# Hybrid decoder step with routed experts on one core: output products by column halves, the first expert's rows picked by TensorE products

## What is computed

```python
x = x + merged @ w['w_out']
hn = rms_norm(x, w['norm_ffn_g']).reshape(B * S, D_MODEL)
x = x + hier_moe(hn, ...)         # every token goes to the best 2 experts of the best of 4 groups
# hier_moe, per expert e, on the rows sent to it:
#   yp = (silu(xb @ w_gate[e]) * (xb @ w_up[e])) @ w_down[e]
#   out[token] += yp * weight of (token, expert)
```

## Time and profile before

| | |
|---|---|
| median of 3 runs | 1033.21 us (1033.18 to 1034.37) |
| the profiled execution | 1037.51 us |
| its span, first to last instruction | 1035.7 us |
| PE busy | 903.2 us, 87% of the span |
| DVE, ACT, POOL busy | 365.3, 224.0, 85.9 us |
| read from HBM, written | 252.46 MB, 14.58 MB |

### The profile page before, as it was taken

One profiled execution on the slowest core, in us unless ns is written; L12 is line 12 of the kernel. 1 busy time (PEld: TensorE's weight loads), 2 busy tenths in 40 slices (PEclk: granted clock), 3 DMA queues, 4 the chain that ended last, 5 costly groups with the idle time before them and its releaser, 6 DMA issues.

```text
span 1035.7 us, 11180 instructions
## 1 busy us (share of the span) xinstructions
PE 903.2 (87%) x4299; PEld 507.1 (49%) x4299; DVE 365.3 (35%) x806; ACT 224.0 (22%) x570; POOL 85.9 (8%) x89
## 2 busy tenths in 40 slices
PE   6899799999899999999859999787877788778784
PEld 5454677777678888755423433232332333233331
DVE  4588568767353345534414111111110101111010
ACT  3432354364622100032201111000010100001010
POOL 0100000000000000000011122010111011010111
PEclk9999899999999999999959999989999999999998
DMA  8622212112112228096369999999999999999991
GB/s 309 205 82 85 77 41 84 46 42 82 41 41 81 82 82 275 1 396 284 125 250 405 389 395 394 388 415 395 404 398 406 407 401 408 402 413 397 411 395 47
DMA packets 34095, 258.46 MB, mean 250 GB/s; under 512 B 9000, under 2 KB 12328, under 8 KB 18792
## 3 DMA queue, kind: packets, MB, share of 16 engines
q1 hardware_dynamic: 28000, 244.93, 59.4%
q0 software_dynamic: 6048, 12.89, 4.7%
HBM read 252.46 MB, written 14.58 MB: 258 GB/s over the span
## 4 chain that ended last, share of the span: by engine, by line
PE 55%; DMA 26%; DVE 7%; issue 6%; ACT 4%; SPq 1%; another core or an unknown queue 1%; POOL 0%; POOLq 0%; DVEq 0%; ACTq 0%
DMA arena<-in_w_gu 19%; PE ps L1723 19%; PE ps L1996 12%; PE ps L2015 7%; PE ps L1662 6%; DMA arena<-in_w_ed 5%; PE ps L1880 4%; PE ps L1985 2%; DVE arena L1289 1%; ACT arena L825 1%; DVE a_stat L1315 1%; DMA arena<-in_x_T 1%; DVE arena L1312 1%; DMA hn_rows<-arena 1%; ACT arena L837 1%
## 5 line engine op out<-in xcount | busy, mean ns | idle before, releaser
L1723 PE MATMUL ps<-arena 128*128 128x272 f32 x1120 | 269.4, 397 | 13.4 <-ACT arena L725 5.8
L1996 PE MATMUL ps<-arena 128*64 128x512 f32 x512 | 232.8, 603 | 19.7 <-DMA arena<-in_w_gu 19.5
L1723 PEld LDWEIGHTS ps<-arena 128*128 128x128 f32 x1120 | 209.9, 191 | 65.1 <-ACT arena L725 11.5
L1997 PE MATMUL ps<-arena 128*64 128x512 f32 x512 | 233.0, 603 | 0.0
L2015 PE MATMUL ps<-arena 128*64 128x512 f32 x512 | 134.6, 673 | 57.2 <-issue 44.0
L725 ACT ACTIVATE arena<-ps 128x272 f32<-128x272 f32 (+5 forms) x172 | 77.2, 457 | 401.5 <-PE ps L2015 175.3
L1996 PEld LDWEIGHTS ps<-arena 128*64 128x64 f32 x512 | 67.0, 138 | 156.1 <-issue 123.8
L1521 DVE SCALAR_TENSOR_TENSOR arena<-ps,list_w,arena 64x512 f32<-64x512 f32 x32 | 23.8, 743 | 286.5 <-ACT arena L990 286.5
L2015 PEld LDWEIGHTS ps<-arena 128*64 128x64 f32 x512 | 43.7, 153 | 145.8 <-issue 137.0
L1662 PE MATMUL ps<-arena 128*128 128x512 f32 (+1 forms) x192 | 75.6, 552 | 8.1 <-DMA arena<-in_w_kv 7.1
L685 POOL DMA_INDIRECT out_y<-arena,list_i x32 | 45.6, 1426 | 402.9 <-PE ps L1985 342.7
(11 more groups left out here) (224 smaller groups left out, 692.1 us busy)
## 6 DMA issues: line engine op xcount, KB each, us to landing
arena<-in_w_gu SPq DMA_DIRECT2D x64, 2048.0 KB, 48.6
arena<-in_w_ed SPq DMA_DIRECT2D x32, 2048.0 KB, 51.2
arena<-in_w_pair SPq DMA_DIRECT2D x20, 1024.0 KB, 4.8
arena<-in_x SPq DMA_DIRECT2D x8, 512.0 KB, 8.2
arena<-in_w_q SPq DMA_DIRECT2D x2, 2048.0 KB, 16.5
arena<-in_w_out SPq DMA_DIRECT2D x2, 2048.0 KB, 13.4
arena<-in_x_T SPq DMA_DIRECT2D x4, 512.0 KB, 8.9
out_y<-arena SPq DMA_DIRECT2D x4, 512.0 KB, 7.0
```

The lines of the kernel that those rows point to most:

```text
L1723: ins = mm(out, w[:, k, :], tokens[:, k, :], start=k == 0 and q in "127", stop=k == 3, skip_group_check=q not in "127")
L1996: mm(ps[0:C, 2 + s, :], xT[s][:, j, :], w[:, jj, 0, :], start=j == 0, stop=j == JX - 1)
L1997: ins = mm(ps[64:64 + C, 2 + s, :], xT[s][:, j, :], w[:, jj, 1, :], start=j == 0, stop=j == JX - 1)
```

## The change

- `w_out` comes as two contiguous column halves. PE does the first column halves of tiles 0 to 3 (h = 1 to 4), then the second halves (h = 5 to 8); the parts of a half are 2, 2 and 4 products (turn, route between them). The routing products of the first halves go to PSUM regions of their own and are kept in `part_logits` (one DVE copy); `choice` adds the second halves' to them.
- The buffer of chunk 7 is the first half of `w_out`: SP loads it when the first halves are done, chunk 8 when all are, chunk 9 after the last rows' transfers. The last tile's write to `hn_rows` moves from POOL's queue to SP's, behind chunk 8. The decode rows of x get a place of their own (part of `const`), so that all of x is loaded beforehand.
- Expert 0's rows are no longer gathered. `hits` makes for each tile a 128x64 table `pick_at` (row r, place p: the row's 1/rms where r belongs at place p of expert 0, else 0), and PE multiplies x by it, 8 products a tile into one PSUM bank that 4 products with a zero row have cleared (`clear_rows`, `pick_rows`). The sum is expert 0's rows, turned and normalised. Counts and the list of weights move to between the two halves of `gate_up(0)`; `turn_x(1)` moves behind `gate_up(0)`; POOL gathers experts 1 and 2 first.

```diff
+        def half_of(h):
+            return ((h - 1) % (NT - 1) + 1, (h - 1) // (NT - 1)) if h else (0, 1)
@@ SP
-            for t in ORDER[:4]:
+            for t in ORDER:
                 load_x(t)
...
-            load_x(ORDER[4])
-            for j in range(1, NT):
-                start_y(j)
-            for n in range(EARLY, N_CHUNK):
-                load_chunk(n)
+            sp.wait_ge(out_ready, half_no(NT - 1, 0) + 1)
+            load_chunk(EARLY)
+            for j in range(1, NT - 1):
+                start_y(j)
+            sp.wait_ge(out_ready, half_no(NT - 1, 1) + 1)
+            load_chunk(EARLY + 1)
+            sp.wait_ge(hn_ready, NT)
+            t = ORDER[NT - 1]
+            sp.dma_start(hn_rows[t * P:t * P + ROWS[t], :], xn[(NT - 1) % 2][0:ROWS[t], :]).then_inc(hn_last, 16)
+            start_y(NT - 1)
+            load_chunk(EARLY + 2)
@@ POOL
-            for e in range(2):
-                gather_x(list_i[:, e:e + 1], e)
+            pool.wait_ge(xe_ready, 1)
+            pool.wait_ge(rows_listed, 1)
+            gather_x(list_i[:, 1:2], 1)
+            gather_x(list_i[:, 2:3], 0)
@@ DVE
+                ts(first_scale[0:r, t:t + 1], one_hot_bf[0:r, t, 0:1], stat[0:r, 2, t:t + 1], None, ALU.mult)\
+                    .then_inc(pick_scaled, 1)
...
+                ts(pick_at[t][0:r, :], cc("place")[0:r, :], ps[0:r, 7, t * NE:t * NE + 1], first_scale[0:r, t:t + 1],
+                   ALU.is_equal, ALU.mult).then_inc(picked, 1)
...
             for j in range(1, NT):
                 add_out(j, 0)
-                choice(j - 1)
                 half_mean(j)
+                if j == 1:
+                    choice(0)
+                if j == 3:
+                    hits(0)
+            for j in range(1, NT):
                 add_out(j, 1)
...
                 inverse2(j)
-                hits(j - 1)
-            choice(NT - 1)
+                if j > 1:
+                    hits(j - 1)
+                choice(j)
             hits(NT - 1)
+            take_x(0, 0)
             dve.wait_ge(list_ready, 1)
@@ PE
+            def pick_rows(j, *js):
+                t = ORDER[j]
+                pe.wait_ge(picked, j + 1)
+                rows = x[t][0:r, :].rearrange("c (p j) -> c j p", j=JX)
+                for jj in js:
+                    ins = mm(ps[:, 0, jj * C:(jj + 1) * C], rows[:, jj, :], pick_at[t][0:r, :], start=False, stop=True,
+                             skip_group_check=True)
-            for j in range(1, NT):
-                half_out(j, 0, 0)
-                turn(2 * j - 2)
-                half_out(j, 0, 1)
-                route(2 * j - 2)
-                if j > 1:
-                    tile_list(j - 2)
-                half_out(j, 1, 0)
-                turn(2 * j - 1)
-                half_out(j, 1, 1)
-                route(2 * j - 1)
-                tile_ranks(j - 1)
+            for h in range(1, 2 * NT - 1):
+                half_out(h, (0, 1))
+                turn(h - 1)
+                half_out(h, (2, 3))
+                if h > NT + 1:
+                    tile_ranks(h - NT - 1)
+                route(h - 1)
+                half_out(h, (4, 5, 6, 7))
+                if h == 3:
+                    tile_ranks(0)
+                if h == 5:
+                    tile_list(0)
+                if h == 7:
+                    tile_list(1)
+                    clear_rows()
+                    pick_rows(0, 0, 1, 2, 3)
+            pick_rows(0, 4, 5, 6, 7)
             turn(2 * NT - 2)
+            tile_ranks(NT - 2)
+            pick_rows(1, 0, 1, 2)
             route(2 * NT - 2)
+            pick_rows(1, 3, 4, 5, 6, 7)
+            tile_list(2)
+            pick_rows(2, *range(JX))
             tile_list(NT - 2)
+            pick_rows(3, *range(JX))
             tile_ranks(NT - 1)
+            pick_rows(NT - 1, *range(JX)).then_inc(xe_ready, 1)
             tile_list(NT - 1)
```

More of the change, by code:

```diff
@@ L215, in build @@
         d_probs = area(11968, 4, 256)
-        w_out = area(0, KD, D)
+        w_out = [area(4096 * c, KD, 512) for c in range(2)]
         x_at = [area(8192 + s * D, D) for s in range(4)]
-        x = [x_at[0], x_at[1], x_at[2], x_at[3], x_at[3]]
+        x = x_at + [const[:, CONST["cos"][0]:CONST["cos"][0] + D]]
+        pick_at = [const[:, CONST["before"][0] + t * C:CONST["before"][0] + (t + 1) * C] for t in range(NT)]
+        zero_row = area(50304 + (NT - 1) * (NG + NE), P)
         pick = area(12288, 2, NT, 2, NE)
         hit = area(12928, 2, NT, C)
-        xn = [area(at, D) for at in (13568, 48256)]
+        xn = [area(at, D) for at in (48256, 13568)]
         w_route = area(14592, KD, NG + NE)
@@ L1460, in hits, with take_x @@
                 tt(hit[0:r, :, t, :], across(cc("place")[0:r, :], 2), over(rank[0:r, :, t], C), ALU.is_equal).then_inc(hit_ready, 1)
+            def take_x(e, s):
+                dve.wait_ge(xe_ready, e + 1)
+                tt(xT[s], split(ps[:, s, :], (JX, C)), over(g_ffn[:, 1, :], C), ALU.mult).then_inc(xe_taken, 1)
             dve.wait_ge(gffn_in, 16)
@@ L1575, in list_items @@
                 dve.tensor_copy(n_item_i[:], total).then_inc(item_ready, 1)
-            take_x(0, 0)
             step(0, 0, 0)
@@ L1905, in route @@
                     pe.wait_ge(x2T_last, 1)
-                j, c = (h + 1) // 2, (h - 1) % 2
+                j, c = half_of(h)
                 t = ORDER[j]
-                above(pe, logits_taken, j)
-                for k in range(KD) if h == 0 else range(4 * c, 4 * c + 4):
-                    rows = dec_x2T[:, k, :] if h == 0 else x2T[c][:, k % 4, :]
-                    ins = mm(ps[0:ROWS[t], 6, t * 36:(t + 1) * 36], rows, w_route[:, k, :], start=k == 0, stop=k == KD - 1)
+                above(pe, logits_taken, j if c == 1 else 1)
+                if h >= NT:
+                    pe.wait_ge(first_logits, 1)
+                at = 36 * t if c == 1 else 36 * (NT + t)
+                ks = range(KD) if h == 0 else range(4 * c, 4 * c + 4)
+                for k in ks:
+                    rows = dec_x2T[:, k, :] if h == 0 else x2T[(h - 1) % 2][:, k % 4, :]
+                    ins = mm(ps[0:ROWS[t], 6, at:at + 36], rows, w_route[:, k, :], start=k == ks[0],
+                             stop=k == ks[-1])
                 ins.then_inc(logit_ready, 1)
@@ L1968, in list_rows, with list_weights @@
                 ins.then_inc(list_ready, 1)
-            pe.wait_ge(hit_ready, NT + 1)
-            list_rows(ps[0:C, 4, 0:NE], 1, 1)
+            def list_weights():
+                for t in range(NT):
+                    r = ROWS[t]
+                    ins = mm(ps[:, 7, 256:256 + NE], ones_bf[0:r, :], one_hot_bf[0:r, t, :], start=t == 0, stop=t == NT - 1)
+                ins.then_inc(count_ready, 1)
+                pe.wait_ge(hit_ready, NT + 1)
+                list_rows(ps[0:C, 4, 0:NE], 1, 1)
             def before_transposing(sem, value):
@@ L1998, in gate_up @@
                     ins.then_inc(used, 1)
+                    if h == 0 and isinstance(e, int) and e == 0:
+                        list_weights()
             def turn_hid(e, s):
@@ L2021, in step @@
                 s = k % 2
+                if isinstance(e, int) and e == 0:
+                    gate_up(0, 0, up_no(0, 0), 0)
+                    turn_x(1, 1, 16)
+                    return
                 if not last:
-                    turn_x(e + 1, 1 - s, (half + 1 + s) * 16)
-                if not isinstance(e, int) or e > 0:
-                    turn_hid(e - 1, 1 - s)
+                    turn_x(e + 1, 1 - s, (half + 1) * 16)
+                turn_hid(e - 1, 1 - s)
                 gate_up(e, s, up_no(k, 0), more)
-                if not isinstance(e, int) or e > 0:
-                    down(e - 1, 1 - s, down_no(k - 1), more)
-            turn_x(0, 0, 16)
+                down(e - 1, 1 - s, down_no(k - 1), more)
             step(0, 0, 0, 0)
```

89 lines of the change are left out of this document (55 added, 34 removed).

## The result

| | before | after |
|---|---|---|
| median of 5 runs | 1034.37 us (1033.18 to 1038.01) | 1042.56 us (1041.04 to 1044.64) |
| the profiled execution, its span | 1037.51, 1035.7 us | 1042.56, 1040.3 us |
| last half ends, last turn starts | 509.72, 511.09 us | 513.88, 515.92 us |
| `gate_up(0)` starts | 535.21 us | 537.29 us |
| chunks 10, 11, 12 go | 540.59, 544.02, 551.20 us | 542.80, 548.32, 556.94 us |

The changed kernel is slower: the ratio of the times is 1.0073, with a 95% interval of 1.0053 to 1.0093. The forecast was 1026.2 us, faster, in 1021.5 to 1031.5. Both profiled executions lie within their kernel's runs; the one of before is 3.1 us over its median, so the two traces are 5.05 us apart where the medians are 8.2.

The account below looks back on a forecast made before the run. The bound was when the chunk stream starts running without pause. `gate_up(0)` 7.6 us earlier made chunk 12 6.35 us earlier; with 0.7 from the stream, -7.0 us off the 1033.21 median gave 1026.2 us, range 1021.5 to 1031.5.

Parts of the forecast that it names:

- what bounds the kernel: Expert stage: the end follows when the chunk stream starts running without pause; PE savings inside the stage are worth nothing.
- Step 4: Chunk stream from chunk 12 on: 2 us of backlog gone, less idle start 0.6 and one gather 0.6; net 0.7 us gained.
- Step 1: Output products up to the last turn: last half ends at 512.6, last turn starts at 515.2, 4.1 us later than before.
- the wait for DVE: Output products: `choice` stalls PE some 0.3 us in slot 7 and holds the last addition, so the last turn, until 515.2.
- Step 2: Last turn to expert 0: 64 pick passes at about 0.125 us; `gate_up(0)` starts at 527.6 instead of 535.21, 7.6 us gained.
- slower: Rival: strided picks become PE's new line; at 0.3 us a pass, 7 us net slower, 1039 us; chance 0.09.
- nothing: Rival: picks cost 0.22 us a pass and 7.2 us take the gain back, 1033 us; chance 0.08.
- Step 3: `gate_up(0)` to chunk 12: chunk 12 goes at 544.85, including 0.5 for the clock, against 551.2; 6.35 us earlier.
- slow clock: Rival: PE falls to 1.2 GHz before expert 0, costing 2 to 3.5 us; 1028.5 to 1030 us; chance 0.11.
- the idle queue: Chunks 10 to 12 finding the queue empty: 0.6 us start kept; 1.4 us more each if all fixed cost preceded the bytes.

Follow-up runs that it names:

- e1: Changed kernel with picks and transpositions reading 128 neighbouring columns instead of every eighth, weights and gains laid out to match; ratio to the kernel before 1.0026.
- e2: Kernel before with transpositions of gathered rows reading neighbouring columns, weights and gains laid out to match; ratio to the kernel before 1.0.
- e5: e1 with 29 added products of constants, never read, among the picks and in PE's waits; ratio to the kernel before 0.9946.
- e3: Changed kernel without its picks: halves, chunk order and last rows' write on SP kept, expert 0 gathered as before; ratio to the kernel before 0.9965.
- e8: e7 with 66 added products, never read, in PE's waits before expert 0 and around the list of weights; ratio to the kernel before 0.9929.
- e9: e8 with 14 more added products where PE waits for expert 0's silu; ratio to the kernel before 0.9927.
- e10: e5 with 14 more added products where PE waits for expert 0's silu; ratio to the kernel before 0.9942.
- e11: Kernel before with only added products (126, never read) in PE's waits, nothing of the change; ratio to the kernel before 1.0002.
- e12: e9 without chunk 9's wait for expert 0's gather, added products kept; ratio to the kernel before 0.9974.
- e7: e3 with chunk 9 issued only when expert 0's gather has landed; ratio to the kernel before 0.996.

## Why the prediction was wrong

**Where the time is decided** (what bounds the kernel, Step 4): right. The stretch from chunk 12 to the end is 483.4 us, forecast within 2 us of 484.5.

**Step 1, the output products:** right but for one term. Clearing and picks ahead of the last half (8 passes each, from 502.19 to 505.12 us) took 2.9 us in place of 2.0, and the second batch of picks, 2.11 us, took the place of the wait for DVE. That the last turn, put at 515.2, came at 515.92 is in part luck: E8 moves by more than that from one execution to the next.

**Step 2, the picks:** this is the step that failed. Its 48 passes, "6.0 us at 0.125", took 12.0 us from start to start, and the 16 more, put at 2.1, took 4.0. The 64 passes lie in one line behind the last turn, as the text says, and so 7.9 us come on. The forecast named this value, 0.25, as its upper bound, and gave "slower" 0.09 and "nothing" 0.08.

The row that I took for it was the wrong neighbour. A pick is a float32 product with a strided stationary operand. The route is a product without the stride (0.114), and the transpositions have the stride but are no product (0.125). e1 and e2 separate these: at full clock a pick pass costs 0.25 with the stride and 0.125 without, a transposition 0.12 with it (8 from 943.31 us to the next product at 944.24) and 0.07 without (940.14 to 940.69). Each of the two rows lacked one of the two factors, and that both lay near 0.12 looked like agreement. The row of transpositions was taken at a clock of 0.50 besides, where e2 shows 0.12 without the stride as well, so it could not have shown what the stride costs. The loads say it plainly: a strided load of a pick takes 335 ns in the median, one of a transposition 203, one of a route 192 (in e5, without the stride, a pick's is 192 too). The Trainium skill has the stride: its page "Advanced Engine Details and Errata", section "Memory Cachelines", has lines of 16 bytes in SBUF and a penalty when each access is to a different one. With float32 words 32 bytes apart every access is; the factor of two at full clock agrees, though the page gives no size. I had not drawn on it, since the 0.125 of the transpositions seemed to show the stride paid for.

**Step 3, the clock:** the second miss. "For the clock I add 0.5." The clock was 0.50 from 517 to 541 us, with no wait of PE over 0.41 us: lists and route took 1.0 us more than reckoned, the first half of `gate_up(0)` 5.5 instead of 3.6 (+1.9), and from chunk 11 to chunk 12 it was 8.6 instead of 7.2 (+1.4); chunk 10 to 11 took 0.5 less. That is the rival "slow clock" on top of "slower". Two readings behind this step were off. The first half of `gate_up(0)` had taken 5.4 us before, not 5.2, and that is 57% more than the second, not 64%. And the clock did not fall "while PE still did turn, route, list and ranks": PE had stopped at 514.25 us and the clock fell at 514.7. The forecast held the slow clock to be an alternative to its own number of 0.125; e1 shows that it also sets the price of the pass. Without the stride the 64 passes still cost 13.9 instead of 8 us in e1, mostly at half clock, so that kernel, too, would have been mispredicted.

**The sum.** Chunk 12 was forecast at 544.35 before the allowance for the clock, and went at 556.94, 12.6 us later: 0.7 from the last turn, 7.9 from the passes, 1.0 from route and lists, 1.9 - 0.5 + 1.4 behind them, and 0.2 of rounding. Behind chunk 12 the stream gave 1.1 us back, where step 4 had reckoned 0.7. So the span came at 1040.3, 11.6 us over the forecast of 1028.7. The median came 16.4 us over its forecast: 4.3 us more since the saving was taken off a median that lay that far below the profiled execution (1037.51 against 1033.21), while the changed kernel's profiled execution is its median, and 0.5 us outside the span.

**Step 4, the idle queue:** the section of the Trainium skill that it leans on is about transfers that GpSimd issues, while chunks 10 to 12 go on SP's queue. No loss of 1.4 us shows behind chunk 12. The bytes of chunk 10 began to move 0.8 us after its issue in both traces (541.4 after 540.59, 543.6 after 542.80), where step 4 has 0.6.

**Right beside this:** the halves and the chunks' new order gain by themselves (e3, -0.35%); the last rows' write lands in 4.4 us at 523.0; the order of arrival was as said, PE behind picks last and DVE done 7.45 us earlier; and the price in "nothing", 0.22 a pass, is near where the change turns into a loss: e1 with 0.23, and the other costs of the low clock, is 0.26% slower than before.

**Best version.** e8 and e9 (halves and chunk order, expert 0 gathered with chunk 9 behind it, PE kept at work) beat both kernels: 1027.83 us against 1035.43 for the kernel before in the same job, -0.7%. With the picks, e5 reaches -0.5% and e10 -0.6%; the intervals of e8 and e10 overlap, so which way is better is open.

## What to carry to other kernels

Price a new instruction by a row that shares every property with it: kind, operand layout and clock. Two rows that each share half of them bound nothing, however well they agree; multiply their factors or take the upper bound. Where a line of small products is to replace a wait, reckon it at the half clock until a trace shows otherwise, since a busy PE is no promise of a fast one. And take causes away together before giving one of them up: stride and clock here, gather and clock in e8, each hid the other.

## What the runs showed of the hardware

- A float32 product's pass whose stationary operand is every eighth word (128 columns) takes 0.25 us at either clock, with 32 rows as with 128; with neighbouring words 0.125 at full clock and 0.23 at half. A transposition's pass follows the same pattern at half the price: 0.12 with the stride at either clock, without it 0.07 at full clock and 0.12 at half (e2).
- The granted clock fell from 1.00 to 0.50, 2.4 to 1.2 GHz, while PE's record was busy 100% of the time (512 to 520 us of the changed kernel) with picks and route, and for 3.2 us in e1 behind clearing and picks. That its array stood waiting for loads (PEld was busy 3.00 of 3.00 us there) is my reading and was not measured. Added products among unstrided picks held it at 1.00; among strided picks the same ones did not.
- From E8 to expert 0 the same code takes 21.3 us mostly at the low and 15.0 at the full clock (e1, e5), with 29 products more in the shorter one.
- After a wait of PE the clock fell late: in e11 and e12 it was still 1.00 through waits of 1.74 and 2.28 us and fell 1.5 and 2.5 us after they ended, among transpositions and the first products of `gate_up(0)`. Behind a wait of 1.9 us for silu it stayed at 1.00 in e3 and was 0.50 in e7.
- E8 moved over 4.3 us between two executions of code that is the same up to there (e5, e10), while in all traces the span followed chunk 12 within 3 us. What moves it was not tried.
